# Chunk recurrence of a hybrid decoder layer: 64x64 products in pairs over the array's four quarters, sample products beside the inverse's first products

## The reference, cut to what matters

```python
def step(S, inp):
    r_t, w_t, k_t, v_t, kk_t, a_t = inp
    sa = jnp.einsum('bhvk,bhk->bhv', S, -kk_t)
    S = (S * w_t[:, :, None, :] + sa[..., None] * (kk_t * a_t)[:, :, None, :]
         + v_t[..., None] * k_t[:, :, None, :])
    return S, jnp.einsum('bhvk,bhk->bhv', S, r_t)
```

## Time and profile before

| | us |
|---|---|
| median of 3 runs | 2431.82 (2431.14 to 2432.91) |
| the profiled execution | 2433.47 |
| its span, first to last instruction | 2431.6 |
| TensorE matmul busy | 2399.4 |
| VectorE busy | 1462.1 |
| ScalarE busy | 985.8 |
| GpSimd busy | 83.1 |

### The profile page before, as it was taken

How to read it: one execution, slowest core, us unless ns; L and a number is a source line. 1 busy time by engine, 2 the same in 40 slices (tenths; PEclk the granted TensorE clock), 3 DMA queues, 4 the chain that set the end, 5 groups by cost and what they waited for, 6 DMA issues and landing times.

```text
span 2431.6 us, 57913 instructions
## 1 busy us (share of the span) xinstructions
PE 2399.4 (99%) x23350; PEld 2367.8 (97%) x23350; DVE 1462.1 (60%) x1996; ACT 985.8 (41%) x1270; POOL 83.1 (3%) x137
## 2 busy tenths in 40 slices
PE   8999999999999999999999999999999999999999
PEld 7999999999999999888999999999999999999999
DVE  6555455545557486667555586766555455555554
ACT  5333333333334544455222345644343334333333
POOL 0000000000003000000000000021000000000000
PEclk9999999999999998899999999999999999999999
DMA  6666566555556744333322444755555555555555
GB/s 237 206 226 205 178 226 235 183 180 181 179 164 218 230 162 150 108 122 132 127 81 83 166 167 137 244 187 178 184 179 183 181 181 181 182 182 182 181 167 172
DMA packets 123044, 428.26 MB, mean 176 GB/s; under 512 B 14345, under 2 KB 20617, under 8 KB 122001
## 3 DMA queue, kind: packets, MB, share of 16 engines
q1 hardware_dynamic: 117504, 393.49, 48.7%
q0 software_dynamic: 5392, 32.61, 4.0%
HBM read 415.17 MB, written 21.33 MB: 180 GB/s over the span
## 4 chain that ended last, share of the span: by engine, by line
PE 92%; DVE 3%; ACT 2%; DMA 1%; DVEq 1%; issue 1%; SPq 0%; ACTq 0%
PE bank L263 29%; PE bank L264 28%; PE bank L265 28%; PE bank L1236 4%; DVE wlo L236 2%; ACT whi L230 1%; DMA raw<-in_weights 1%; PE bank L1398 0%; ACT rkv L662 0%; PE bank L1565 0%; PE bank L1436 0%; DMA x<-in_x 0%; PE bank L1584 0%; PE bank L1577 0%; DVE kkey L1070 0%
## 5 line engine op out<-in xcount | busy, mean ns | idle before, releaser
L236 DVE TENSOR_TENSOR wlo<-raw,whi 128x1024 fp32r<-128x1024 f32 (+3 forms) x794 | 914.9, 1155 | 652.9 <-ACT whi L230 650.4
L263 PE MATMUL bank<-hhi,whi 128*128 128x264 f32 x4048 | 1168.0, 289 | 12.7 <-DVE hlo L299 12.1
L264 PE MATMUL bank<-hlo,whi 128*128 128x264 f32 x4048 | 1151.6, 284 | 0.0
L230 ACT ACTIVATE whi<-raw 128x1024 fp32r<-128x1024 f32 (+3 forms) x794 | 793.1, 1001 | 882.5 <-PE bank L265 862.5
L265 PE MATMUL bank<-hhi,wlo 128*128 128x264 f32 x4048 | 1150.4, 284 | 0.0
L263 PEld LDWEIGHTS bank<-hhi,whi 128*128 128x128 f32 x4048 | 767.0, 189 | 24.4 <-DMA ones<-in_ones 12.1
L264 PEld LDWEIGHTS bank<-hlo,whi 128*128 128x128 f32 x4048 | 767.3, 190 | 0.9
L265 PEld LDWEIGHTS bank<-hhi,wlo 128*128 128x128 f32 x4048 | 763.5, 189 | 0.0
L263 PE MATMUL bank<-mhi,whi 128*128 128x264 f32 x1408 | 399.5, 284 | 0.0
L265 PE MATMUL bank<-mhi,wlo 128*128 128x264 f32 x1408 | 398.9, 283 | 0.0
L264 PE MATMUL bank<-mlo,whi 128*128 128x264 f32 x1408 | 398.9, 283 | 0.0
(11 more groups left out here) (270 smaller groups left out, 1777.0 us busy)
## 6 DMA issues: line engine op xcount, KB each, us to landing
raw<-in_weights SPq DMA_DIRECT2D x666, 512.0 KB, 3.3
raw<-in_weights SPq DMA_DIRECT2D x64, 384.0 KB, 3.1
out_skv<-in_cache POOLq DMA_DIRECT2D x16, 512.0 KB, 3.8
raw<-in_weights SPq DMA_DIRECT2D x32, 256.0 KB, 2.8
raw<-in_weights SPq DMA_DIRECT2D x32, 192.0 KB, 2.4
side<-stg POOLq DMA_DIRECT2D x18, 132.0 KB, 3.6
gates<-side POOLq DMA_DIRECT2D x1, 2376.0 KB, 13.7
x<-in_x SPq DMA_DIRECT2D x4, 528.0 KB, 6.6
```

Of the source, the lines that this page charges most:

```text
L230: act.activation(whi[:, u % RING, 0:n], raw[:, u % RING, 0:n], ACT.Copy).then_inc(hi_done, 1)
L236: dve.tensor_tensor(wlo[:, s, 0:n], raw[:, s, 0:n], whi[:, s, 0:n].bitcast(F32), ALU.subtract).then_inc(lo_done, 1)
L263: pe.matmul(bank[:, 0:T], hi, xhi[:, k], start=(k == 0), stop=False)
L264: pe.matmul(bank[:, 0:T], hi, xlo[:, k], start=False, stop=False)
```

## The change

Every product is given straight or crossed so that two of them with different banks can be issued in turn, in all four quarters. `per_head` now takes any number of products and returns the last matmul of each; `per_head_twice` is gone. A result that was summed in one go (w1, y, the state) is now summed by matmuls that stand at different places: `first` clears the bank at its first matmul only and `last` closes it.

- First stretch of a chunk: tm/qm's pair, then b*a with k*a. Second stretch: b*r with v's transpose, k*r with b's transpose. VectorE masks the first halves of ab and ak together (`aa_out`), after tm and qm, and the second halves later (`ar_out`).
- Levels 2, 3, 4: the sample product (`removed`, `added`, `removed`) stands beside m1, and `sample_u`, `sample_v` ahead of the level's additions on VectorE. The second `added` of a chunk still stands alone, at level 5.
- Level 5: m1 with ak*vt, the addition to qm with a*state; w1 is complete with the latter.
- um with state*r; after a gates quarter and um's copy um*ab with kt*vt (`two_pe`); the sample reads; then vt*ak with bt*um, which complete y and the state; only then the last quarter of the gates block.

```diff
-            dve.wait_ge(ab_pe, c + 1)
-            for q in range(2):
-                ins_ = dve.tensor_tensor(ab[:, 4 * q:4 * q + 4], A4[q][:].rearrange("p (j n) -> p j n", n=2 * C),
-                                         over(cc("causal"), 4), ALU.mult)
-            ins_.then_inc(ab_out, 1)
             dve.wait_ge(tq_pe, c + 1)
             dve.tensor_tensor(tm[:], by_head(A4[2]), over(cc("join0t"), PAIRS), ALU.mult)
             dve.tensor_tensor(qm[:], by_head(A4[3]), over(cc("join0"), PAIRS), ALU.mult).then_inc(tq_out, 1)
+            dve.wait_ge(aa_pe, c + 1)
+            dve.tensor_tensor(ab[:, :, 0:C], by_head(A4[0]), over(cc("causal", 0, C), PAIRS), ALU.mult)
+            dve.tensor_tensor(ak[:, :, 0:C], by_head(A4[1]), over(cc("causal", 0, C), PAIRS), ALU.mult).then_inc(aa_out, 1)
...
             for lv in range(1, 6):
+                if lv == 3:
+                    sample_v(2 * c)
+                elif lv in (2, 4):
+                    sample_u(2 * c + (lv - 2) // 2)
                 dve.wait_ge(add_pe, 5 * c + lv)
...
-        def head(j, p, bank, width, col0, terms, frm, to):
-
-            out = bank(j)[half(p ^ to), col0(j):col0(j) + width]
-            for t, (lhs, rhs) in enumerate(terms):
-                mm = pe.matmul(out, lhs(j, p ^ frm), rhs(j, p ^ frm), start=(t == 0), stop=(t == len(terms) - 1))
-            return mm
+        def head(j, p, bank, lhs, rhs, frm=0, to=0, first=None, last=None):
+
+            return pe.matmul(A4[bank][half(p ^ to), C * j:C * j + C], lhs(j, p ^ frm), rhs(j, p ^ frm),
+                             start=first is None or (first and j == 0), stop=last is None or (last and j == PAIRS - 1))
...
+        def per_head(*products):
+
+            ends = [None] * len(products)
             for j in range(PAIRS):
-                for product in (a, b):
+                for i, product in enumerate(products):
                     for p in range(2):
-                        mm = head(j, p, *product)
-            return mm
+                        ends[i] = product(j, p) if callable(product) else head(j, p, *product)
+            return ends
...
             if c:
+                pe.wait_ge(st_out, c)
+                pe.wait_ge(sy_out, c)
+            per_head((2, a_, b_), (3, b_, a_, 0, 1))[1].then_inc(tq_pe, 1)
+            if c:
                 pe.wait_ge(um_out, c)
                 pe.wait_ge(y_out, c)
...
+            per_head((0, b_, a_), (1, k_, a_, 0, 1))[1].then_inc(aa_pe, 1)
             block_pe("gates", b, (0, 1))
...
             pe.wait_ge(tq_out, c + 1)
-            per_head(one(2), C, c64, (v_, ident))
-            per_head(one(3), C, c64, (b_, ident)).then_inc(tr_pe, 1)
+            pe.wait_ge(aa_out, c + 1)
+            per_head((0, b_, r_), (2, v_, ident, 0, 1))
+            ar, tr = per_head((1, k_, r_, 0, 1), (3, b_, ident))
+            ar.then_inc(ar_pe, 1)
+            tr.then_inc(tr_pe, 1)
             block_pe("gates", b, (2, 3))
...
+                    m1_end, su = per_head(m1_of, removed(2 * c))
+                    m1_end.then_inc(m1_pe, 1)
+                    su.then_inc(su_pe, 1)
...
+                    per_head(m1_of, (2, part(ak), part(vt), 1, 1, True, False))[1].then_inc(m1_pe, 1)
...
+                    pe.wait_ge(state_done, c + 1)
+                    add, w = per_head(add_q, (2, a_, part(state), 0, 1, False, True))
+                    add.then_inc(add_pe, 1)
+                    w.then_inc(w1_pe, 1)
...
-            per_head(one(0), C, c64, (part(qm), part(w1)), frm=1).then_inc(um_pe, 1)
+            per_head((0, part(qm), part(w1), 1, 0), (1, part(state), r_, 0, 0, True, False))[1].then_inc(um_pe, 1)
             block_pe("gates", b + 3, (2,))
+            pe.wait_ge(um_out, c + 1)
+            per_head((1, part(um), part(ab, C), 0, 0, False, False), (2, part(kt_), part(vt), 1, 0, True, False)
+                     )[1].then_inc(two_pe, 1)
             pe.wait_ge(pair_done, 2 * c + 2)
...
             mm.then_inc(sy_pe, 1)
+
+            pe.wait_ge(two_pe, c + 1)
+            y, st_new = per_head((1, part(vt), part(ak, C), 1, 0, False, True), (2, part(bt), part(um), 0, 0, False, True))
+            y.then_inc(y_pe, 1)
+            st_new.then_inc(st_pe, 1)
             block_pe("gates", b + 3, (3,))
-            pe.wait_ge(um_out, c + 1)
-            per_head(one(1), C, c64, (part(state), r_), (part(um), part(ab, C)), (part(vt), part(ak, C))).then_inc(y_pe, 1)
-            pe.wait_ge(kt_out, c + 1)
-            per_head(one(2), C, c64, (part(bt), part(um)), (part(kt_), part(vt))).then_inc(st_pe, 1)
```

More of the change, by code:

```diff
@@ L1143, in chunk_dve @@
             to_spill(b - 1)
[L1144 to L1148, removed]
+            dve.wait_ge(ar_pe, c + 1)
+            dve.tensor_tensor(ab[:, :, C:], by_head(A4[0]), over(cc("causal", C, C), PAIRS), ALU.mult)
+            dve.tensor_tensor(ak[:, :, C:], by_head(A4[1]), over(cc("causal", C, C), PAIRS), ALU.mult).then_inc(ar_out, 1)
             zm_of(2)
@@ L1158, in chunk_dve @@
                 lo("gates", b + (1 + lv) // 2, (1 + lv) % 2)
[L1159 to L1165, removed]
+                if lv in (1, 3):
+                    to_spill(b + lv // 2)
+                elif lv == 5:
+                    sample_v(2 * c + 1)
             to_spill(b + 2)
@@ L1492, in chunk_pe @@
             a_, r_, b_, k_, v_ = (part(buf, at) for buf in (kkey, R_, iclr, K_, V_))
[L1493 to L1496, removed]
             pe.wait_ge(prep, RT)
@@ L1522, in chunk_pe @@
                 if lv == 1:
[L1523 to L1530, removed]
-                add_q = (one(1), C, c64, ((part(m1), part(qm)),), 1, 1)
-                if lv == 1:
-                    pe.wait_ge(vb_out, c + 1)
-                if lv < 5:
-                    mm = per_head_twice(add_q, (one(2), C, c64, ((part(qm), part(m1)),), 1, 0))
-                else:
-                    mm = per_head(*add_q[:3], *add_q[3], frm=1, to=1)
-                mm.then_inc(add_pe, 1)
-                if lv == 1:
-                    per_head(one(3), C, c64, (k_, ident)).then_inc(kt_pe, 1)
+                    pe.wait_ge(ar_out, c + 1)
+                m1_of = (0, part(zm[lv % 2]), part(tm), 0, 1)
+                if lv == 1:
+                    per_head(m1_of)[0].then_inc(m1_pe, 1)
                 elif lv == 2:
@@ L1567, in chunk_pe @@
             mm.then_inc(sy_pe, 1)
+            pe.wait_ge(two_pe, c + 1)
+            y, st_new = per_head((1, part(vt), part(ak, C), 1, 0, False, True), (2, part(bt), part(um), 0, 0, False, True))
+            y.then_inc(y_pe, 1)
+            st_new.then_inc(st_pe, 1)
             block_pe("gates", b + 3, (3,))
[L1569 to L1572 removed]
         def removed(j):
[L1575 to L1586 removed]
+            return lambda s, p: pe.matmul(
+                A4[3][half(p), s * HD:s * HD + HD], kkey[half(p), j, SEQ + s:SEQ + s + 1].to_broadcast([HD, HD]),
+                sst[half(p), j, s], start=True, stop=True)
+        def added(j):
+            return lambda s, p: pe.matmul(
+                A4[3][half(p), s * HD:s * HD + HD], V_[half(p), j, SEQ + s:SEQ + s + 1].to_broadcast([HD, HD]),
+                ident(j, p), start=True, stop=True)
         block = ctx.enter_context(nc.Block())
```

58 lines of the change are left out of this document (23 added, 35 removed).

## The result

| us | before | after |
|---|---|---|
| median | 2432.36 (2431.14 to 2433.84, 4 runs) | 2397.22 (2393.68 to 2399.24, 4 runs) |
| profiled execution | 2433.47 | 2393.68 |
| its span | 2431.6 | 2391.7 |

What follows compares the result with a forecast made beforehand. The prediction took TensorE's own stream as the bound (99% busy, no idle in chunks 1 and 2). Its terms, 40.8 + 0.36 - 0.3 - 2.0 = 38.8 us saved, gave a forecast of 2393.0 us, range 2389.5 to 2400.

Steps and rivals of the forecast that it cites:

- The second product of a pair is free: TensorE's 64x64 stretches: a straight and a crossed product together take 1.09 us, as long as a lone product's 1.08.
- 11 slots gone: TensorE per chunk: turns of 16 matmuls at 0.93 us fall from 32 to 21, saving 10.2 us, 40.8 in four chunks.
- The fewer stretches: Chunk boundaries: only the last chunk's extra run of 64x64 products disappears, gaining 0.36 us once.
- Rival (b): New pairs run one after the other: 2433 us, no change, or 2422 by the skill page; chance 0.04 for both.
- VectorE's cover in the levels: Chunk levels of 5.46 us instead of 6.39: VectorE may be 0.1 to 0.2 late once, with 1.1 us of cover remaining.
- Rival (a): Some wait becomes real in every chunk (VectorE's middle levels, state add, masks): 7.2 us in all, 2400; chance 0.12.
- The thinnest cover: VectorE's y copy and state add before the next chunk: cover 0.1 to 0.2 us, charged 0.3 for three chunks.
- Chunk 0: First chunk: longer mask wait and low clock lose 2.0 us of the saving, bounds 0.5 and 3.5.
- The wait for the masks: Chunk 0: TensorE arrives earlier while VectorE masks four operations instead of two, so it idles 4.3 us from 1153.0.
- My walk: Step through a steady chunk of 47.8 us, checking when each engine finishes; TensorE was to be never idle.
- rival d: TensorE's two clock dips become two more or one fewer: 2396 or 2389.5; counted within the forecast's 0.80.
- Rival (c): Granted clock held at 0.5 over the chunks: 140 us slower, 2533 in all; chance 0.03.

Runs made afterwards that it cites:

- experiment 1: Changed kernel with two loops in `per_head` swapped, so a pair's products are issued one after the other instead of in turn: 2433.83 us, ratio to before 1.0011.
- experiment 9: The changed kernel run once more, unedited, for the spread between executions: 2395.23 us, ratio to before 0.9867.
- experiment 2: Changed kernel with the sample products of levels 2 to 4 issued behind m1 instead of beside it: 2401.46 us, ratio to before 0.9884.
- experiment 4: Changed kernel with a third gates block ahead of the chunks and the first block's store ahead of the samples' state load: 2394.13 us, ratio to before 0.986.
- experiment 3: Changed kernel with three gates blocks instead of two ahead of the chunks: 2397.91 us, ratio to before 0.9874.

## Why the prediction was right, and where it missed

**The second product of a pair is free: right.** The new pairs take 1.09, and experiment 1 shows that it is the order in which they are issued that does it. 11 slots gone were to save 40.8 in four chunks; with the stops taken out a chunk takes 47.85 as forecast (47.8), which saves 40.8. The fewer stretches gave 0.44 for 0.36. Rival (b) is out.

**VectorE's cover in the levels: right.** Its busy time stayed at 33.3 a chunk, a level lasted 5.48 (1231.38 to 1236.86 in the chain) for the 5.46 expected, and no wait of TensorE's names VectorE after chunk 0. Rival (a) is out. The thinnest cover, y and the state under one quarter, held: no wait of its own shows there. I had put 0.3 on it; it cost nothing.

**Chunk 0: the mechanism right, the term too small.** The wait for the masks was sized rightly. I expected 4.3 us of idle; experiment 9, with no stop ahead of it, had 4.3, and here 3.7 and a stop of 0.6 before it make the same, 2.2 more than before. But the low clock behind it lasted 6.8 us and cost 2.2, where before's cost 1.5 and mine, on two slots, was to cost less than before's four. In the last stretch a stop of 0.6 came on top of the second low clock (2.0 together for 1.5). 2.2 + 0.7 + 0.5 is 3.4 of the 3.6 lost, where I had 2.0 and an upper bound of 3.5. The low clock was worked out as if it came back as soon as before, for which the earlier trace rows gave no reason.

**The term that was missing: the supply of instructions.** My walk said that TensorE would never be idle in a steady chunk. It counted engines, semaphores, queues of data and the clock, but not how fast the instructions come. Halving the time of a product doubles the rate at which they are used: 256 in 1.86 us. It cost 2.1 us in chunks 1 to 3 and 0.6 in chunk 0, whose first stop only shortened the wait behind it. In the chunks of before no stop showed, though the pairs of additions stood in it: each was alone among lone products and quarters, while now two pairs follow one another at a chunk's start, where the stop of 1249.19 lies, and most quarters have a pair on both sides. The 117 transfers on the instruction queue were on the page, and I passed over them.

**The sum.** 38.8 + 0.1 (stretch) + 0.3 (no tight wait) - 1.6 (chunk 0) - 2.1 (stops) = 35.5, the 35.56 of the profiles. The median came out 4.2 above the forecast: 3.3 from this sum, 0.5 because before's median was 2432.36 when timed beside it, and 0.4 between profiles and medians. The number of the clock's dips (rival d) stayed at two. Its figure for one dip fewer was wrong by its own price: at 1.4 us it is 2391.6 and not 2389.5, which changes nothing in the comparison. Rival (c), a low clock over the chunks, didn't come: 0.91 in chunk 0 and 1.00 behind it.

**What stays open.** Why a transfer of instructions starts when it does, and so why the stops at the same place last 0.84 us in one kernel and 1.89 in another. And what decides on the low clock: an idle of 2.1 us had it behind it before, one of 3.0 in experiment 1 did not, one of 3.7 had 3.4 us of it in experiment 2 and 6.8 in the changed kernel, and in experiment 4 it followed a stop of 1.04. That a version without stops would be quicker by their sum was not shown, because none of the runs was without them and with pairs.

## What to carry to other kernels

Two products of which one uses the straight and the other the crossed quarters of the array cost as much as one, if their matmuls are issued in turn; one behind the other the second costs about 0.7 of 0.93 us. Before a term is made out of "half the slots", divide the instructions of the densest stretch by its new time and set that beside the rate of the instruction queue, for a queue that the page shows at 0.3% can still be late. A wait that the change lets TensorE reach sooner costs its own length and a low clock behind it, and when it is taken away its price may come back at the next engine's queue (experiment 3) or at the next stop (experiment 4).

## What the hardware showed that was not expected

- TensorE's stream has stops of 0.3 to 3.3 us that no semaphore explains. In nine executions all 51 of over 0.4 us stand at the same place modulo 256 of TensorE's instructions (173 to 175), and added instructions move them by their own number (64 by 64 to 66, 128 by 126 to 130). They were seen in the chunks of every kernel that issues the new pairs in turn, in none of the two that don't.
- TensorE goes on 2.2 to 2.9 us after the start of a 16384-byte transfer on the instruction queue and 1.2 to 1.6 after its end, however long it stood. A stop's length follows from how late that transfer starts; the longest, 3.33 us, had one that started 1.0 after TensorE had stopped.
- Matmuls of two products in four quarters start 0.0145 us apart; of one product in two quarters 0.029.
- Of products issued one after the other in different quarters, the second begins before the first is done, which saves 0.18 us of its 0.93 in the stretch shown and 0.23 on the mean of a chunk.
- 3.0 us without a matmul left the clock at its upper level in one kernel; behind 3.7 us it was low for 3.4 us in a second and for 6.8 in a third.
